# The order of value loads and key loads in the attention steps of a hybrid decoder layer

## What is computed

```python
# mixer A: 8 heads x 64, keys gathered by stride from a window cache of 2048 positions
for window, dil in ((128, 1), (512, 4), (2048, 16)):
    o, lse = dilated_gather_attention(aq, kcat, vcat, dil, window // dil)
a_out = merge_by_denominator(outs, lses)
# mixer B: 4 heads, two softmaxes over 2048 paged positions, 16 pages of 128
past_k = pool_k[page_table].reshape(b, PAST_LEN, B_HEADS, 2, HEAD_DIM)
past_v = pool_v[page_table].reshape(b, PAST_LEN, B_HEADS, B_VDIM)
attn = a[:, :, 0] - lam * a[:, :, 1]
b_out = einsum('bhqk,bkhe->bqhe', attn, v)
```

## Time and profile before

| what | value |
|---|---|
| median of 2 runs | 1681.38 us (1679.64 to 1683.11) |
| the profiled execution's own time | 1686.0 us |
| its span in the trace | 1684.2 us |
| TensorE busy (matmul) | 1534.2 us, 91% of the span |
| VectorE busy | 667.2 us, 40% |
| ScalarE busy | 513.7 us, 31% |
| GpSimd busy | 66.1 us, 4% |
| mean granted clock of TensorE | 0.958 |
| DMA | 245.71 MB, mean 146 GB/s |

### The profile page before, as it was taken

How to read it: one execution, slowest core, us unless ns; L and a number is a source line. 1 busy time by engine, 2 the same in 40 slices (tenths; PEclk the granted TensorE clock), 3 DMA queues, 4 the chain that set the end, 5 groups by cost and what they waited for, 6 DMA issues and landing times.

```text
span 1684.2 us, 31988 instructions
## 1 busy us (share of the span) xinstructions
PE 1534.2 (91%) x12575; PEld 1341.7 (80%) x12575; DVE 667.2 (40%) x1333; ACT 513.7 (31%) x835; POOL 66.1 (4%) x162
## 2 busy tenths in 40 slices
PE   4899999999998999888898878877899999999996
PEld 3788999999996777655565555547789999999996
DVE  0322323322426423354554545645643232332343
ACT  2411222221214121244444444443342222221122
POOL 0200000000002000000000000000010000000000
PEclk9999999999998999989999999988989999999998
DMA  9993232232222141478888998873212222233211
GB/s 331 389 333 123 75 87 78 84 99 86 72 71 83 50 131 63 123 218 264 264 264 270 256 273 246 271 228 96 73 45 81 87 75 87 77 99 86 85 54 57
DMA packets 215906, 245.71 MB, mean 146 GB/s; under 512 B 9023, under 2 KB 152889, under 8 KB 215810
## 3 DMA queue, kind: packets, MB, share of 16 engines
q1 hardware_dynamic: 215810, 244.42, 46.9%
HBM read 237.31 MB, written 7.08 MB: 145 GB/s over the span
## 4 chain that ended last, share of the span: by engine, by line
PE 40%; SPq 8%; issue 3%; DMA 3%; DVE 3%; ACT 2%; ACTq 0%; DVEq 0%
PE ps L288 27%; SPq L1170 4%; SPq L1147 4%; PE ps L1256 3%; DMA kv<-in_cache_diff_k_dram 3%; PE ps L272 2%; PE ps L1268 1%; PE ps L1312 1%; PE ps L1330 1%; PE ps L952 1%; PE ps L1355 1%; PE ps L1295 1%; DVE VH L1571 1%; DVE xT L312 1%; DMA kv<-in_cache_win_v_dram 0%
## 5 line engine op out<-in xcount | busy, mean ns | idle before, releaser
L257 ACT ACTIVATE whi<-w 128x1024 fp32r<-128x1024 f32 (+1 forms) x152 | 171.1, 1128 | 741.5 <-PE ps L288 641.9
L263 DVE TENSOR_TENSOR wlo<-w,whi 128x1024 fp32r<-128x1024 f32 (+1 forms) x152 | 200.4, 1319 | 422.3 <-ACT whi L257 422.0
L288 PE MATMUL ps<-hhi,whi 128*128 128x288 f32 x1440 | 310.7, 297 | 3.7 <-ACT tmp L653 3.7
L288 PE MATMUL ps<-hlo,whi 128*128 128x288 f32 x1440 | 308.9, 296 | 0.0
L288 PE MATMUL ps<-hhi,wlo 128*128 128x288 f32 x1440 | 308.7, 296 | 0.0
L288 PEld LDWEIGHTS ps<-hhi,whi 128*128 128x128 f32 x1440 | 232.2, 189 | 9.2 <-issue 4.8
L288 PEld LDWEIGHTS ps<-hlo,whi 128*128 128x128 f32 x1440 | 232.8, 189 | 0.0
L288 PEld LDWEIGHTS ps<-hhi,wlo 128*128 128x128 f32 x1440 | 232.5, 189 | 0.0
L1256 PEld LDWEIGHTS ps<-ident,kv 128*128 128x128 f32 (+1 forms) x896 | 101.7, 149 | 88.9 <-issue 65.4
L1256 PE MATMUL ps<-ident,kv 128*128 128x128 f32 (+1 forms) x896 | 126.1, 283 | 46.0 <-DMA kv<-in_cache_diff_k_dram 33.2
L288 PE MATMUL ps<-ffhi,whi 128*128 128x288 f32 x704 | 151.2, 296 | 0.0
(11 more groups left out here) (197 smaller groups left out, 1684.8 us busy)
## 6 DMA issues: line engine op xcount, KB each, us to landing
w<-in_ffn_w_in_dram SPq DMA_DIRECT2D x88, 512.0 KB, 3.8
wada<-in_w_ada_dram SPq DMA_DIRECT2D x18, 2048.0 KB, 13.8
kv<-in_cache_diff_k_dram SPq DMA_DIRECT2D x128, 256.0 KB, 4.0
kv<-in_cache_diff_v_dram SPq DMA_DIRECT2D x128, 256.0 KB, 3.6
w<-in_ffn_w_out_dram SPq DMA_DIRECT2D x32, 704.0 KB, 4.6
w<-in_w_qkv_dram SPq DMA_DIRECT2D x24, 512.0 KB, 3.7
kv<-in_cache_win_k_dram SPq DMA_DIRECT2D x32, 384.0 KB, 5.1
kv<-in_cache_win_v_dram SPq DMA_DIRECT2D x32, 384.0 KB, 7.6
```

Of the source, the lines that this page charges most:

```text
L257: nc.scalar.activation(whi[:, slot, 0:w], w32[:, slot, 0:w], ACT.Copy).then_inc(ph.hi, 1)
L263: nc.vector.tensor_tensor(wlo[:, slot, 0:w], w32[:, slot, 0:w], whi[:, slot, 0:w].bitcast(F32), ALU.subtract).then_inc(ph.lo, 1)
L288: m = pe.matmul(ps[:, banks + h, 0:TH], w, x[:, kk, h * TH:(h + 1) * TH], start=(kk == 0 and n == 0), stop=(kk == kall - 1 and n == 2))
```

## The change

In `attend_sync`, within each step, the value load of the quarter five steps back is issued ahead of this step's key load. The loads themselves, their waits, slots and sizes stay as they are.

```diff
--- before.py
+++ after.py
@@ -1176,8 +1176,6 @@
 
             def body(b, run):
                 for i in quarters(b):
-                    if alive(b) and (b, i) not in ((0, 0), (0, 1)):
-                        load(b, i, 0)
                     if isinstance(b, int) and b == 0 and i == 1:
 
                         eng.wait_ge(sem("qk_turned"), 4 * (PT_ + 1))
@@ -1187,6 +1185,8 @@
                     vb, vi = back(b, i, LAG)
                     if alive(vb):
                         load(vb, vi, 1)
+                    if alive(b) and (b, i) not in ((0, 0), (0, 1)):
+                        load(b, i, 0)
 
             each_sequence(body)
```

## The result

The changed kernel takes 1739.88 us (two runs, 1739.70 and 1740.07) against 1681.38: ratio 1.0358, 95% interval 1.0325 to 1.0392. It is 58.5 us slower. The profiled execution after took 1739.7 us (span 1737.9), the one before 1686.0 (span 1684.2), so 53.7 of the 58.5 us can be read in the two traces; the rest is that the profiled execution of before stood 4.6 us above its median.

What follows compares the result with a forecast made beforehand. Bound: attention, SP's chain of page reads and load issues, then a key landing. A cycle of 56.5 against 51.96 us gives 31.8 over seven; plus 1.2 and 1.3 makes +34.3, 1715.7 us; range 1684 to 1740, likeliest case 1703 to 1727.

Steps and rivals of the forecast that it cites:

- X2: End of the value products of step 2 on TensorE, put at 37.9 us after step 5's start.
- T7 to T1: TensorE's start of step 7 to start of step 1: 13.1 us, with a new 3.4 us wait before step 1.
- Rival (b): SP's chain is the bound and gets shorter by covered page reads: some 5 us less, 1676 us; chance 0.12.
- K1: Key load of step 1, taken to land 6.8 us after its second DMA begins.
- T5 to T7: TensorE's start of step 5 to start of step 7, put at 13.6 us.
- K7: Key load of step 7: landed at 12.8 us after step 5's start, hidden as step 7 starts at 13.6.
- K6: Key load of step 6: lands 4.5 us after its last DMA begins, so step 6 starts at 8.5.
- T1 to T4: TensorE's start of step 1 to start of step 4, put at 22.6 us.
- rival (c): New stall before step 1 halves the clock there: +2 to +3 us per cycle, some +50, 1731; chance 0.14.
- K4: Key load of step 4: last DMA at 43.8 us after step 5's start, landing 5.5 us later.
- rival (a): Transfers served strictly in order, so K4 lands in 3.6 us despite the value load behind: +21, 1702; chance 0.24.
- T4 to T5: TensorE's start of step 4, now the stalled step, to start of step 5: 7.2 us.

Runs made afterwards that it cites:

- light value loads: Changed kernel with every value DMA from sequence 1 on bringing only 16 of its 96 or 128 rows: 1723.05 us; same edit on the kernel before: 1678.48 us.

## Why the prediction was right and where it was wrong

**Direction and mechanism: right in the main.** The forecast was slower, by 34.3 us on the profiled execution. It was 53.7 there and 58.5 in the medians. That the total lies inside the range is luck: it is at the very upper end (1739.88 of 1740). The chances put "within 2%" (0.52) above slower (0.46), which was wrong. The chain is in the trace: the stall before step 5 is gone, one of 4.4 to 8.0 us at the lower clock stands before step 4, V7 goes out as X2 ends, and V1 waits up to 6.6 us for X4. The stall before step 1 is there in sequences 1 to 3 (3.4 to 4.1 us) and in 6 (1.1), not in 4, 5 and 7. In 4 and 5 a stall of 1.5 and 2.9 us stands before step 0 instead, which the forecast didn't have; by its own last sentence ("wrong if step 1 starts without a wait") it fails in these sequences, though T7 to T1 is 12.7 and 15.0 there. Rival (b), not slower, is out: K1 never landed within 3.4 us.

**What failed is the sum of the cycle: one term put at nothing and three that were mis-sized.** By the table, the forecast is short in each part, and most where it had put nothing:
- T5 to T7: 1.1 us. The step that failed is "landed at 12.8 by the 3.6: hidden under T7 = 13.6". K7's slowest DMA landed in 4.0 to 5.1 us, and the value products of step 5, for which V2 ahead of it waits, ended 5.2 to 6.0 us after T5 instead of 4.8. The room was 0.8 us; step 7 stalled 0.2 to 1.0 us in six of the seven cycles. Keys first in steps 7 and 0 gives back 0.6. The rest is the cycle that starts in sequence 4 (17.2 us): K6, for which 0.6 was put in, stalled step 6 by 4.1 us, and that step then ran at the lower clock for a part. The stalls before step 6 of sequence 4 and step 7 of sequence 5:

```profile
989.49 1.21 PE L1256 MATMUL ps<-ident,kv 128*128 128x128 f32 x8 [4.12 <-DMA kv<-in_cache_diff_k_dram]
...
1056.82 1.09 PE L1256 MATMUL ps<-ident,kv 128*128 128x128 f32 x8 [1.04 <-DMA kv<-in_cache_diff_k_dram]
```

- T7 to T1: 0.9, of which the forecast had 0.2 outside its cycle (the 1.2 us for sequences 6 and 7). K1's second DMA was to go out 6.3 us after T7 and went out after 6.3 to 7.4, 6.7 in the mean, as V4's four DMAs took SP 1.9 to 2.8 us instead of 1.95. It landed in 7.0 in the mean instead of 6.8.
- T1 to T4: 0.5. Here it is T1 to X2 that was short, 11.8 us for 11.2. Step 1 ran at the lower clock behind its stall in sequences 1 to 3, where T1 to T2 is 8.7, 9.7 and 8.8 us for 7.8; this was rival (c)'s mechanism. From X2 to T4 the forecast's 11.4 us is right (11.3), but by two errors of opposite sign: K4's last DMA went out 6.3 us after X2 instead of 5.9, and it landed in 4.7 instead of 5.5. That is halfway to rival (a)'s 3.6, and the time is far from its 1702. Its rule from the Trainium skill ("DMA: Bandwidth & Descriptors", Queues, rings and completion order) is that a DMA engine consumes descriptors in ring order, by which the bytes of V0 behind K4 should cost K4 nothing. The light value loads agree with that (4.8 us with a sixth of V0 behind K4, 4.7 with all), but K4 still took 0.9 more with V0 right behind it than the 3.8 without, and no run here shows why.
- T4 to T5: 0.4.

That is 2.9 us per cycle, 20 us over seven; less the 1.2 that the forecast had added apart, and with 0.4 more in sequence 0, it is the gap of 19.4 us on the profiled executions. The range of the likeliest case (22 to 46 us more) was too narrow; the bounds of the single terms, taken together, reach 59 and hold the result.

**The offset.** The forecast kept the 4.6 us by which the profiled execution of before stood above its median. After the change that distance is 0 (1739.7 against 1739.88), which makes up the other 4.8 of the 58.5 us. The medians of before in the later runs lie between 1681 and 1685, so it is within what runs differ by.

**What in the change costs.** Three things were put in front of each key load. The value load's wait alone, on the order of before, makes 0.6 us per cycle in the traces and 11.8 us in the medians. The bytes of the value loads give back 16.8 us in the changed order when most of them go, but 3.6 (not clear of the noise) in the order of before too, so some 13 to 17 us of the 58.5 come with the change. The page reads give back 26 us in the changed order, but 21 in the order of before, and with both treated alike the change still costs 52 us. So page reads are a cost of both orders, in other places, and not what makes the changed one slower. What remains is the key load's place behind the value load's wait and its issue together; no run splits that further.

**The steps don't add.** Alone, step 1 costs 25 us, step 4 9, steps 5 and 6 20, steps 7 and 0 22, steps 2 and 3 nothing: 76 in all, where the whole change costs 58.5. Steps 1 to 6 together already have the whole cycle of 59.5 us.

## What to carry to other kernels

When a load is moved behind another on the same issuing queue, it inherits that one's wait, its issue time and its bytes. Look also at the scalar work on that queue, such as reading page numbers: read them once, and put them where the engine really waits. In the changed order reads ahead of a wait gave 26 us; in the order of before, where SP wasn't waiting at that place, they gave nothing. To say that such work is what a change costs, take it out of both kernels and compare again. A stall found in front of one step is no measure of slack in front of the next if the issuing engine's own waits restart behind it; follow each wait to the next issue that depends on it. And when a term is called hidden, write down how much room it has: K7 had 0.8 us and needed more.

## What the runs showed that was not expected

A paged key load takes 3.6 to 4.4 us to its last byte as K4 and 4.7 to 6.8 as K5 in the order of before (sequences 1 to 7). In the changed order K4 takes 4.0 to 6.4 and K5 4.3 to 6.6. With a sixth of the value loads' rows K5 of the order of before takes 4.1 to 5.4, so bytes are a part of it. What makes the rest was not found.

The lower clock can come some time after a stall, so the first transposes don't tell. In the changed kernel, step 1 of sequence 1 started at full speed behind a stall of 4.07 us, and its second eight transposes took 1.49 us:

```profile
770.78 0.88 PE L1256 MATMUL ps<-ident,kv 96*128 96x96 f32 x8 [4.07 <-DMA kv<-in_cache_win_k_dram]
...
773.25 1.49 PE L1256 MATMUL ps<-ident,kv 96*128 96x96 f32 x8
```

The granted clock was 0.50 from 772.8 to 774.8 us. Step 1 of sequence 2 had 1.54 us for its first eight, behind a shorter stall (3.42 us), and 0.50 at once.
